# Router logits in one wide product per chunk, and another order of small PE work around the last projection group

## What is computed

```python
def _moe(h, router, wg, wu, wd):
    xt = h.reshape(-1, D_MODEL)
    logits = (xt @ router).astype(jnp.float32)
    top_v, top_i = lax.top_k(logits, TOP_K)
    top_w = jax.nn.softmax(top_v, axis=-1)
    ...
    for e in range(N_EXPERTS):
        y = y + gates[:, e:e + 1] * _swiglu(xt, wg[e], wu[e], wd[e])
```

## Time and profile before

| | before |
|---|---|
| median of 3 runs | 1505.51 us (1504.45 to 1506.86) |
| the profiled execution | 1503.68 us, of which span 1501.9 us |
| granted TensorE clock, mean over the span | 0.994 |
| PE busy | 1459.6 us (97%) |
| DVE, ACT, POOL busy | 1095.7, 877.5, 147.7 us |
| moved by DMA | 378.05 MB, 252 GB/s on average |

### The profile page before, as it was taken

How to read it: one execution, slowest core, us unless ns; L and a number is a source line. 1 busy time by engine, 2 the same in 40 slices (tenths; PEclk the granted TensorE clock), 3 DMA queues, 4 the chain that set the end, 5 groups by cost and what they waited for, 6 DMA issues and landing times.

```text
span 1501.9 us, 26668 instructions
## 1 busy us (share of the span) xinstructions
PE 1459.6 (97%) x11549; PEld 1203.7 (80%) x11549; DVE 1095.7 (73%) x1029; ACT 877.5 (58%) x868; POOL 147.7 (10%) x179
## 2 busy tenths in 40 slices
PE   6999999999999988999999999999999999999997
PEld 6999999999979977877767777777777777777774
DVE  5687455554378964223698898888988888888897
ACT  4445443433366623342577777777777777777775
POOL 0056100000200041232300000000000000000110
PEclk9999999999999999999899999999999999999999
DMA  7653564545335120144799999999999999999991
GB/s 232 198 156 96 157 226 162 165 126 156 102 106 177 57 59 5 35 139 164 263 355 402 387 369 380 382 377 392 365 376 386 374 390 365 367 388 371 393 405 62
DMA packets 250317, 378.05 MB, mean 252 GB/s; under 512 B 28217, under 2 KB 142121, under 8 KB 249906
## 3 DMA queue, kind: packets, MB, share of 16 engines
q1 hardware_dynamic: 247922, 370.04, 69.2%
q0 software_dynamic: 2064, 6.18, 1.2%
q10 hardware_dynamic: 208, 0.07, 0.0%
HBM read 368.47 MB, written 7.78 MB: 251 GB/s over the span
## 4 chain that ended last, share of the span: by engine, by line
PE 94%; DVE 3%; issue 1%; ACT 1%; DMA 0%; ACTq 0%; DVEq 0%
PE bank L2656 48%; PE bank L2020 29%; PE bank L2333 1%; PE bank L2315 1%; PE bank L2563 1%; PE bank L2588 1%; PE bank L2665 1%; PE bank L2073 1%; PE bank L2503 1%; PE bank L2143 1%; PE bank L2511 1%; DMA vecrows<-b_w 0%; PE bank L2193 0%; DVE wL L1700 0%; PE bank L2647 0%
## 5 line engine op out<-in xcount | busy, mean ns | idle before, releaser
L1700 DVE TENSOR_TENSOR wL<-ering,wH 128x2048 fp32r<-128x2048 f32 x263 | 602.7, 2296 | 82.1 <-ACT wH L1166 80.7
L1166 ACT ACTIVATE wH<-ering 128x2048 fp32r<-128x2048 f32 x264 | 505.9, 1917 | 141.9 <-PE bank L2656 141.7
L2656 PE MATMUL bank<-wH,xgH 128*96 128x512 f32 (+1 forms) x768 | 290.0, 378 | 0.5 <-DVE wL L1700 0.5
L2656 PE MATMUL bank<-wL,xgH 128*96 128x512 f32 (+1 forms) x768 | 287.2, 374 | 0.0
L2656 PE MATMUL bank<-wH,xgL 128*96 128x512 f32 (+1 forms) x768 | 287.1, 374 | 0.0
L2656 PEld LDWEIGHTS bank<-wH,xgL 128*96 128x96 f32 x768 | 124.5, 162 | 44.0
L2656 PEld LDWEIGHTS bank<-wH,xgH 128*96 128x96 f32 x768 | 124.5, 162 | 43.5 <-issue 1.5
L2656 PEld LDWEIGHTS bank<-wL,xgH 128*96 128x96 f32 x768 | 124.6, 162 | 41.6
L2656 PE MATMUL bank<-wH,hH 128*96 128x512 f32 x352 | 139.7, 397 | 0.3 <-DVE wL L1700 0.3
L2656 PE MATMUL bank<-wH,hL 128*96 128x512 f32 x352 | 138.3, 393 | 0.0
L2656 PE MATMUL bank<-wL,hH 128*96 128x512 f32 x352 | 137.9, 392 | 0.0
(11 more groups left out here) (462 smaller groups left out, 2599.2 us busy)
## 6 DMA issues: line engine op xcount, KB each, us to landing
ering<-m_w_gate SPq DMA_DIRECT2D x88, 1024.0 KB, 7.2
ering<-m_w_up SPq DMA_DIRECT2D x88, 1024.0 KB, 7.6
ering<-m_w_down SPq DMA_DIRECT2D x88, 1024.0 KB, 7.4
arena<-a_w_in SPq DMA_DIRECT2D x16, 1024.0 KB, 5.4
arena<-b_w_rkv SPq DMA_DIRECT2D x12, 1024.0 KB, 5.1
fring<-f_w_gate SPq DMA_DIRECT2D x11, 1024.0 KB, 5.0
fring<-f_w_up SPq DMA_DIRECT2D x11, 1024.0 KB, 5.0
fring<-f_w_down SPq DMA_DIRECT2D x16, 704.0 KB, 4.4
```

Of the source, the lines that this page charges most:

```text
L1166: s_.activation(wH[:, hslot(g), :], ering[:, eslot(g), :], ACT.Copy).then_inc(S["e_hi"], 1)
L1700: v.tensor_tensor(wL[:, hslot(g), :], ering[:, eslot(g), :], wH[:, hslot(g), :].bitcast(F32), ALU.subtract).then_inc(S["e_lo"], 1)
L2656: mm = t.matmul(dst, lhs[l], rhs[r], start=(start and m == 0), stop=(stop and m == 2), skip_group_check=True)
```

## The change

Three things change, all in the code shown above.

`row_logits` swaps its operands: the router's chunk (128x8) becomes the weight, and all 288 tokens stream, so a chunk needs one matmul (two instructions) in place of three (six), and the logits come out transposed, 8 rows of 288. DVE copies them to `lgT` (a new instruction, in the unused `hS`), PE transposes them back in three tiles to columns 320 and on of bank 4, and the selection reads them there. `r_logit` is counted three times for it.

`row_logits(6)` and the first three of four blocks of each of the row transposes 3, 4 and 5 move from behind the last projection group to before it; the fourth blocks stay behind. Transposes 5 go to bank 2 instead of 3, since bank 3 is the last group's.

The norm sums move from behind the places to before them, and to bank 3.

```diff
--- before.py
+++ after.py
@@ -298,6 +298,8 @@
         SwT = view(CHN + 6848, T, parts=CAP)
         got = (rows2[:, 0, :], rows2[:, 1, :], ytk_rest)
         LAST = E_ - 1
+        LOGIT = 320
+        lgT = hS[0:E_, 0, 0:T]
         psel = eview(rbase + 368, 48, "p (i k e) -> p i k e", i=3, k=2)
         tsel = eview(rbase + 416, 48, "p (i k e) -> p i k e", i=3, k=2)
 
@@ -543,7 +545,7 @@
         UP_AT = (2, 6, 10, 14, 18, 21)
         ADD_AT = (14, 17, 20, 23, 26, 29)
 
-        ROWS_AT = (5, 6, 7, 0, 1, 3)
+        ROWS_AT = (5, 6, 7, 0, 1, 2)
         FIRST_AT = (2, 6, 7, 5)
 
         def main(rd):
@@ -1215,7 +1217,7 @@
             row_copy(4)
             act.wait_ge(S["norm_sum"], 3)
             for rows, lo, hi in ((P, 0, 2), (SMP, 2, 3)):
-                s_.activation(lnT[0:rows, lo:hi], banks[2][0:rows, lo:hi], ACT.Ln, bias=eps[0:rows, 0:1],
+                s_.activation(lnT[0:rows, lo:hi], banks[3][0:rows, lo:hi], ACT.Ln, bias=eps[0:rows, 0:1],
                               scale=1.0 / D).then_inc(S["rms_ready"], 1)
             act.wait_ge(S["rms_ready"], 4)
             for rows, lo, hi in ((P, 0, 2), (SMP, 2, 3)):
@@ -1734,11 +1736,13 @@
 
             dve.wait_ge(S["r_const"], 12)
             dve.wait_ge(S["r_logit"], 1)
+            v.tensor_copy(lgT, banks[4][0:E_, 0:T]).then_inc(S["r_logit"], 1)
+            dve.wait_ge(S["r_logit"], 3)
             for i, (_, n) in enumerate(TILES):
-                step(v.max(out=top[0:n, i, 0:8], in_=banks[4][0:n, 8 * i:8 * i + 8]))
+                step(v.max(out=top[0:n, i, 0:8], in_=banks[4][0:n, LOGIT + 8 * i:LOGIT + 8 * i + 8]))
             steps_done()
             for i, (_, n) in enumerate(TILES):
-                step(v.max_index(out=topi[0:n, i, 0:8], in_max=top[0:n, i, 0:8], in_values=banks[4][0:n, 8 * i:8 * i + 8]))
+                step(v.max_index(out=topi[0:n, i, 0:8], in_max=top[0:n, i, 0:8], in_values=banks[4][0:n, LOGIT + 8 * i:LOGIT + 8 * i + 8]))
             steps_done()
             link(v.tensor_copy(topf[:, :, 0:2], topi[:, :, 0:2]))
             for k, dst in ((0, oh1), (1, oh2)):
@@ -2566,18 +2570,17 @@
                             mm.then_inc(S["wo_ready"], 1)
             def row_logits(c):
                 pe.wait_ge(S["xt_ready"], 3 * DC + c + 1)
-                for i, (t0, n) in enumerate(TILES):
-                    mm = t.matmul(banks[4][0:n, 8 * i:8 * i + 8], xT[:, c, t0:t0 + n], router[:, c, :],
-                                  start=(c == 0 and i == 0), stop=(c == DC - 1), skip_group_check=True)
-                return mm
-
-            def row_transposes(n):
+                return t.matmul(banks[4][0:E_, 0:T], router[:, c, :], xT[:, c, :],
+                                start=(c == 0), stop=(c == DC - 1), skip_group_check=True)
+
+            def row_transposes(n, blocks=range(4)):
                 i, q = n % 3, n // 3
                 t0, rows = TILES[i]
-                pe.wait_ge(S["xt_ready"], 3 * DC + 4 * q + 4)
-                for j in range(4):
+                pe.wait_ge(S["xt_ready"], 3 * DC + 4 * q + blocks[-1] + 1)
+                for j in blocks:
                     mm = t.transpose(banks[ROWS_AT[n]][0:rows, P * j:P * j + P], xT[:, 4 * q + j, t0:t0 + rows], ident[:, :])
-                mm.then_inc(S["h_tr"], 1)
+                if blocks[-1] == 3:
+                    mm.then_inc(S["h_tr"], 1)
 
             pe.wait_ge(S["r_const"], 10)
             for q in range(2, 4):
@@ -2593,10 +2596,24 @@
                         row_logits(2 * c - 7)
                     if c < DC - 1:
                         row_transposes(c - 4)
-            row_logits(DC - 2)
+                    if c == DC - 2:
+                        row_logits(c)
+                        for n in range(3, 6):
+                            row_transposes(n, range(3))
             row_logits(DC - 1).then_inc(S["r_logit"], 1)
             for n in range(3, 6):
-                row_transposes(n)
+                row_transposes(n, range(3, 4))
+            pe.wait_ge(S["r_logit"], 2)
+            for i, (t0, n) in enumerate(TILES):
+                mm = t.transpose(banks[4][0:n, LOGIT + 8 * i:LOGIT + 8 * i + 8], lgT[:, t0:t0 + n], ident[0:E_, 0:E_])
+            mm.then_inc(S["r_logit"], 1)
+            pe.wait_ge(S["sq_sum"], 3 * (DC - 2))
+            pe.wait_ge(S["sq_ready"], 3 * DC)
+            for c in (0, DC - 1):
+                for i, (t0, n) in enumerate(TILES):
+                    mm = t.matmul(banks[3][0:n, i:i + 1], sq3[:, c, t0:t0 + n], ones[:, 0:1],
+                                  start=(c == 0 and i == 0), stop=(c > 0), skip_group_check=True)
+            mm.then_inc(S["norm_sum"], 1)
             pe.wait_ge(S["r_sel"], 1)
             first = True
             for i, (_, n) in enumerate(TILES):
@@ -2607,14 +2624,6 @@
                                   start=first, stop=(j == i), skip_group_check=True)
                     first = False
             mm.then_inc(S["r_pos"], 1)
-            pe.wait_ge(S["sq_sum"], 3 * (DC - 2))
-            pe.wait_ge(S["sq_ready"], 3 * DC)
-            for c in (0, DC - 1):
-                for i, (t0, n) in enumerate(TILES):
-                    mm = t.matmul(banks[2][0:n, i:i + 1], sq3[:, c, t0:t0 + n], ones[:, 0:1],
-                                  start=(c == 0 and i == 0), stop=(c > 0), skip_group_check=True)
-            mm.then_inc(S["norm_sum"], 1)
-
             def e_index(rd):
                 pe.wait_ge(S["e_sx"], rd * 6 + 15)
                 for i, (_, rows) in enumerate(TILES):
```

## The result

The changed kernel takes 1508.51 us (median of 20 executions, 1506.18 to 1513.43), the kernel before, run beside it, 1505.42 us (20 executions). The ratio is 1.0021, with a 95% interval of 1.0012 to 1.0030: slower by 3.1 us, at the edge of what I had called measurable.

The account below looks back on a forecast made before the run. TensorE, busy 97% of the span, was taken as the bound, its rigid expert block passing on any later start. Work +0.9 and clock +1.2 gave +2.1 on the median 1505.5, so 1507.6 us, range 1504.8 to 1509.9.

Parts of the forecast that it names:

- slower rival: Clock falls before the places are done, place and one-hot products at half speed: +3.3 us, +4.9 at most; chance 0.30.
- forecast: Structure +0.9 us and a somewhat earlier clock fall +1.2, so +2.1; chance 0.42.
- Steps (1) and (2): Ahead of the last projection group: wide logits save 0.99 us, moved logits and transposes add 1.57; group starts 0.58 later.
- Step (4): Behind the last group: logits copied by DVE (0.45 us) and transposed back (0.53); first maximum 1.58 later in all.
- step (5): Norm sums fit into the selection before the places; one-hot products begin 1.84 us behind places instead of 2.52, gaining 0.68.
- Step (3): Behind the last group: moved work was free there, hidden in waits; PE now idles until chunk 7's logits.
- step (6): Clock falls earlier, 3.8 to 7.5 us behind the last group; the middle of the interval costs 1.2.
- Structure only: Nothing happens to the clock but a shift: +0.9 us (0.4 to 1.2); chance 0.16.
- Faster: Wide logits in the thin stretch keep the clock up: 4.2 us less, with +0.9 makes -3.3; chance 0.12.

Follow-up runs that it names:

- m1_move: Kernel before with only nine blocks of row transposes 3 to 5 moved ahead of the last projection group; 1509.89 us, ratio 1.0044 to before.
- s1_stream: Kernel before with logits of chunks 6 and 7, places and norm sums streaming repeated columns; 1500.63 us, ratio 0.9975 to before (0.9984 when run again).
- c2_after_stream: Changed kernel with places widened to 120 columns and norm sums to 128; 1502.57 us, ratio 0.9989 to before.
- u1_not_moved: Changed kernel with the nine transpose blocks and chunk 6's logits put back behind the last projection group; 1505.95 us, ratio 1.0008 to before.
- n1_narrow: Changed kernel without the wide logits, their copy and transposes back, chunk 6's logits behind the last group again; 1507.19 us, ratio 1.0023 to before.
- s4_places_norm: Kernel before with places and norm sums widened by repeated columns, logits as before; 1501.82 us, ratio 0.9979 to before.
- u2_both: Changed kernel with the move undone, and places widened to 120 and norm sums to 128 columns; 1503.88 us, ratio 0.9984 to before.
- n2_wide_only: Kernel before with the wide logits alone (product, copy, transposes back); 1505.83 us, ratio 1.0013 to before.
- s2_fillers: Changed kernel with extra matmuls that nothing needs in PE's four waits; 1505.68 us, ratio 0.9999 to before.

## Why the prediction was right, and where it was off

The range held the time, and both halves of the mechanism are confirmed: more work ahead of the one-hot products, and an earlier fall of the clock. The size was off by one term, the work: 1.6 for the +0.9 that I had summed. With that the result (+3.1) came nearer to the slower rival's +3.3 than to the forecast's +2.1, though not by that rival's mechanism. And it is within the range because that rival set its upper end.

Steps (1) and (2), logits. The sum set a chunk's wide logits at 2 x 0.2425 and called this an upper bound, which it was not. In the trace a pair of chunks costs 1.16 instead of 0.97, since PE loses 0.09 when it turns from 128-column weights to the 8-column ones and 0.09 when it turns back. The three pairs saved 0.42 instead of 0.99, and chunk 6, with both turns for itself, cost 0.67 (718.45 to 719.12) instead of 0.49. The transposes came out about as summed (1.04 for 1.08). Together 1.3 instead of 0.58: this is the term that was mis-sized, by 0.7. Step (4) gave back 0.3 of it and step (5) added 0.2.

Step (3), that the moved work was free where it stood: right for the time, and m1_move is its direct proof, with a 1.27 us wait in its place. For the clock it was not free, which step (6) covers only as a thinner stretch.

Step (4), the detour: 0.73 longer instead of 1.0. Copy 0.45, as taken from the 128x288 copy; the three 8-row transposes take 0.31 together, not 0.53.

Step (5): the norm sums fit, as forecast. The gain was 0.47 instead of 0.68; the first one-hot product starts 0.31 behind the end of its matrix, not 0.1.

Step (6), the clock: +1.2 in the one-hot products, and measured 1.2. The interval for the fall (3.8 to 7.5 behind the last group) holds both traces of the changed kernel, 6.1 and 4.9; that the middle of the interval gave the measured 1.2 is partly luck, since the interval stood on one fall elsewhere in the trace. Why the clock falls earlier was left open between two readings. s1_stream and c2_after_stream show that the fall depends on how many columns PE's small products stream behind the last group, and m1_move and u1_not_moved that the nine transposes count as well. The reading by the Trainium skill (TensorE: Matmul & The Clock Gate, Part 4: PE-mode transpose), that transposes don't count for the clock as products do, would have left m1_move's fall where it was before. It came at 5.3 instead of 7.5, and the average clock went from 0.9938 to 0.9910; for 128x128 transposes of 32-bit data in this kernel the measurement decides against it, as far as they would count for nothing. Whether one counts as much as a product of as many columns was not measured.

The rivals. *Slower* by places at half speed is not what the two traces of the changed kernel show (falls at 730.1 and 726.8, with places at 728.0 and 725.8), but it occurred in n1_narrow. *Structure only* is refuted by the traces of the changed kernel, with the one-hot stretch 1.2 to 1.3 longer, and by c2_after_stream, which gains 5.6 us with the same structure and order. *Faster* did not happen by itself; its mechanism is real, and s1_stream is a way to get it. Its sum put the low stretch at 4.2 us; the trace of s1_stream gained 3.2 although its small products took 0.7 longer, so about 3.9.

What stays open: why m1_move, with less work than the changed kernel, loses more by its six executions (the intervals 1.0018 to 1.0048 and 1.0028 to 1.0060 overlap, and by the traces it loses less, 2.3 against 2.9 and 3.0). How thin a stretch must be was not measured either; these runs only order the kernels.

Of the kernels tried, the one before with widened places and norm sums (s4_places_norm, or s1_stream with the logits too) has the lowest ratios to before, 0.9975 to 0.9984, and by 0.9979 / 1.0021 it is some 0.4% under the changed kernel; u2_both (0.9984) can't be told from it.

## What to carry to other kernels

Work that hides in another engine's dependency chain is free there, and may be doing a second job: keeping TensorE's clock up. Before moving it ahead of dense work, look at what the stretch that it leaves still streams. Where small matmuls are bound by their weight loads, streaming repeated columns into unused PSUM cost 0.02 to 0.03 us for each instruction here, and was worth more than the changed order. And price a matmul of a new weight shape with the turn to it and back, not only with its own step.

## What the runs showed of the hardware

- A turn from 128-column to 8-column weights and back costs 0.09 us each way in the trace of after (16 projection instructions hold PE for 3.97 us when 8-column logits follow, instead of 3.88; the four logits instructions take 1.07 when transposes of 128 columns follow, where four steps of 0.2425 make 0.97).
- 12 place instructions with up to 120 columns took 0.20 us more in total than with 8, and 12 norm instructions with up to 128 columns 0.34 more than with 1 (s1_stream against before).
- The granted clock was low for 10.2 us behind the group in the traces of before and n2_wide_only, for about 13.7 in those of the changed kernel (both), m1_move, u1_not_moved and s2_fillers, and for 17.1 in that of n1_narrow, although PE was busy for nearly all of each (13.44 of the 13.5 us from 730.0 in after).
- The clock fell with PE hardly idle: in flight for 7.11 of the last 7.45 us before the fall in before, for 2.87 of 2.92 in n1_narrow.
